# The sample rows' 256 keys chosen on 128 partitions instead of 32, with totals by TensorE and one bank for the attention's sums

## The reference, cut to what matters

```python
score = einsum('bth,bths->bts', wib * IDX_HEADS ** -0.5, relu(idx_s))
score = where(causal, score, NEG)
top_s, top_i = lax.top_k(score, n_sel)             # n_sel = 256
kvs = kv[b_ix, top_i]
s = einsum('btghd,btngd->btghn', qg, kvs[:, :, :, 0]) * scale
p = _masked_softmax(s, ok)
o = einsum('btghn,btngd->btghd', p, kvs[:, :, :, 1])
```

## Time and profile before

| | us |
|---|---|
| runs: median of 3 (lowest, highest) | 2315.91 (2314.22, 2325.44) |
| profiled execution: its own time | 2321.67 |
| profiled execution: its span | 2319.9 |
| PE busy in the span | 1865.5 (80%) |
| DVE busy in the span | 1210.8 (52%) |
| ACT busy in the span | 626.4 (27%) |

### The profile page before, as it was taken

How to read it: one execution, slowest core, us unless ns; L and a number is a source line. 1 busy time by engine, 2 the same in 40 slices (tenths; PEclk the granted TensorE clock), 3 DMA queues, 4 the chain that set the end, 5 groups by cost and what they waited for, 6 DMA issues and landing times. The chain is left out here.

```text
span 2319.9 us, 29122 instructions
## 1 busy us (share of the span) xinstructions
PE 1865.5 (80%) x11577; PEld 1283.2 (55%) x11577; DVE 1210.8 (52%) x2379; ACT 626.4 (27%) x1574; POOL 206.6 (9%) x190
## 2 busy tenths in 40 slices
PE   5589998969999667596899987978867667787595
PEld 2289998336666444384676644554542344444383
DVE  0231002757777652443223899946956998233443
ACT  0331121555666112002111000005633444222101
POOL 0033120000000531000011000000020000331000
PEclk9789999979999877598999999989987999898698
DMA  6321111400000554310111101100010000884301
GB/s 207 155 113 55 57 38 50 161 34 1 1 1 2 243 247 182 147 46 30 62 61 42 48 19 38 38 0 1 1 51 23 1 1 1 322 352 197 147 1 75
DMA packets 38450, 188.53 MB, mean 81 GB/s; under 512 B 8267, under 2 KB 8364, under 8 KB 21738
## 3 DMA queue, kind: packets, MB, share of 16 engines
q0 software_dynamic: 16912, 102.68, 11.3%
q1 hardware_dynamic: 21404, 83.98, 10.0%
HBM read 171.69 MB, written 19.12 MB: 82 GB/s over the span
## 5 line engine op out<-in xcount | busy, mean ns | idle before, releaser
L729 PE MATMUL banks<-hT,w_in 128*128 128x352 f32 x864 | 264.5, 465 | 39.9 <-DVE qdT L801 18.8
L729 PEld LDWEIGHTS banks<-hT,w_in 128*128 128x128 f32 x864 | 163.9, 192 | 138.5 <-DVE qdT L801 21.1
L2471 PE MATMUL banks<-w_out_parts,mix_parts 128*128 128x512 f32 (+1 forms) x864 | 204.8, 400 | 36.1 <-DVE w_out_parts L176 36.1
L2471 PEld LDWEIGHTS banks<-w_out_parts,mix_parts 128*128 128x128 f32 (+1 forms) x864 | 159.8, 186 | 83.5 <-DVE w_out_parts L176 40.4
L1304 ACT ACTIVATE nsa_p<-banks,nsa_negmax 128x512 f32<-128x512 f32 (+3 forms) x192 | 104.2, 557 | 94.0 <-DVE nsa_negmax L1223 94.0
L724 PE MATMUL banks<-hT_rest,w_in_high 128*128 128x352 f32 x384 | 124.0, 323 | 0.0
L724 PE MATMUL banks<-hT_high,w_in_high 128*128 128x352 f32 x384 | 124.0, 323 | 0.0
L724 PE MATMUL banks<-hT_high,w_in_rest 128*128 128x352 f32 x384 | 123.9, 323 | 0.0
L726 PE MATMUL banks<-w_in,hT 128*128 128x256 f32 (+3 forms) x576 | 118.9, 362 | 6.1 <-DMA w_in<-in_w_in 6.1
L1223 DVE TENSOR_REDUCE nsa_negmax<-banks 128x2 f32<-128x1024 f32 (+4 forms) x77 | 84.6, 1099 | 69.7 <-PE banks L1177 59.4
L853 ACT ACTIVATE mix<-banks 128x352 f32<-128x352 f32 x48 | 22.0, 465 | 348.4 <-PE banks L729 229.0
(11 more groups left out here) (525 smaller groups left out, 3566.4 us busy)
## 6 DMA issues: line engine op xcount, KB each, us to landing
w_in<-in_w_in SPq DMA_DIRECT2D x24, 1056.0 KB, 4.9
ada_w<-in_ada SPq DMA_DIRECT2D x24, 1024.0 KB, 4.9
w_out<-in_l_w_out SPq DMA_DIRECT2D x4, 2048.0 KB, 7.7
x_in<-in_x_prompt SPq DMA_DIRECT2D x1, 4096.0 KB, 15.0
nsa_ring<-in_state_l_win_kv POOLq DMA_DIRECT2D x8, 512.0 KB, 6.9
x_after<-in_x_prompt SPq DMA_DIRECT2D x1, 4096.0 KB, 17.8
x_mid<-x_after SPq DMA_DIRECT2D x8, 512.0 KB
x_after<-x_mid SPq DMA_DIRECT2D x1, 4096.0 KB, 17.9
```

The lines of the kernel that those rows point to most:

```text
L729: last = pe.matmul(bank[:, 0:cn], w[:, j % slots, a, m * P:(m + 1) * P], k.hT[:, a, c0:c0 + cn], start=(a == 0), stop=(a == KT - 1))
L2471: last = pe.matmul(k.bank[u % 4][0:n, :], lhs, rhs, start=a == 0 and x == 0, stop=a == KT - 1 and x == 2)
```

## The change

**Layout.** `sample_score` has 128 partitions and 544 columns: the quarter g of the 2048 past keys (512 keys) lies on partitions 32g to 32g+31, and the new keys on the last quarter's columns 512 to 543; the other quarters have -3e38 there. TensorE writes the sums of the heads to the partitions of their quarter (two products of 256 columns for one of 512), and VectorE's copies have 64 partitions and 256 columns.

**The choice** is the class `SampleChoice` in place of `top_mask`. A count runs over 544 columns on 128 partitions and gives a partial count of each quarter. A product with `mates` (1 where two partitions belong to one sample row) puts the sum of the four on every partition, in column 0 of `bank[7]`; VectorE reads it there in its next turn. The equal scores use `earlier` in the last product, so that quarters count the ones before them. `top_mask` stays for the prompt rows.

**The loop.** `attend_pairs` takes `beside` for `between`. With it, there is one bank of sums, `bank[6]`, and a tile's products wait for the close of the tile before. VectorE does the close and the step of the choice at the start of a turn, ahead of the maxima, and TensorE does the total behind the transposes.

```diff
-            k.sample_score = k.sb(ws, "idx_score_s", [NS, PAST + NS], side="right")
+            k.sample_score = k.sb(ws, "idx_score_s", [P, QUARTER + NS], side="right")
...
-            choice = top_mask(k, k.nc.vector, ws, "sample_top", [(k.sample_score[:, :], k.sample_sel[:, :])], TOPK, NS)
-            attend_pairs(k, "dsa", jobs, values, close, scale_heads, dve_copies=None, between=choice)
+            attend_pairs(k, "dsa", jobs, values, close, scale_heads, dve_copies=None, beside=SampleChoice(k, ws, k.bank[7]))
...
+    sums = 1 if beside is not None else 2
+    sum_bank = lambda i: k.bank[6 + i % sums]
...
-                    if i >= 2:
-                        pe.wait_ge(closed, i - 1)
+                    if i >= sums:
+                        pe.wait_ge(closed, i - sums + 1)
...
+                    if beside is not None and t < beside.rounds:
+                        beside.sum_quarters(pe, t)
                     if t - LAG - 1 >= 0:
                         add(t - LAG - 1)
...
+                    if sums == 1 and t - LAG - 2 in ends:
+                        end_tile(t - LAG - 2)
+                    next(steps, None)
                     if t < U:
                         maximum(t)
...
+    def sum_quarters(self, pe, n):
+        pe.wait_ge(self.counted, n + 1)
+        pe.matmul(self.total, (self.earlier if n == self.rounds - 1 else self.mates)[:, :, :].rearrange("p g n -> p (g n)"), self.seen[:, :],
+                  start=True, stop=True).then_inc(self.totalled, 1)
...
+        for bit in range(30, -1, -1):
+            link(dve.tensor_scalar(self.place[:, :], self.found[:, :], 1 << bit, None, ALU.bitwise_or))
+            link(dve.tensor_tensor(self.bits[:, :], self.place[:, :], self.flip[:, :], ALU.bitwise_xor))
+            count_of(ALU.is_ge, self.upper[:, :] if bit >= 16 else score, kth, self.mask[:, :])
+            yield
+            n += 1
+            dve.wait_ge(self.totalled, n)
+            link(dve.tensor_scalar(self.step[:, :], self.total, count, float(1 << bit), ALU.is_ge, ALU.mult))
+            link(dve.tensor_tensor(self.found[:, :], self.found[:, :], self.step[:, :], ALU.bitwise_or))
...
-                    pe.matmul(sum_bank(c)[0:NS, 0:width(c)], wsum[:, :], relu[:, c % 2, 0:width(c)], start=True, stop=True).then_inc(summed, 1)
+                    v = relu[:, c % 2, :].rearrange("k (j p) -> k j p", j=4)
+                    for side in range(2):
+                        quarter = 2 * (c // 2) + side
+                        last = pe.matmul(sum_bank(c)[quarter * NS:(quarter + 1) * NS, 0:256].rearrange("n (j p) -> n j p", j=4), wsum[:, :],
+                                         v[:, :, side * HD:(side + 1) * HD], start=True, stop=True, skip_group_check=True)
```

More of the change, by code:

```diff
@@ L65, in constants @@
     rows["cmp_seen"] = q >= CMP - 1
-    rows["idx_tail"] = NEG * ~((r32 // DS == q // DS) & (r32 % DS <= q % DS))
+    rows["idx_tail"] = NEG * ~((r32 // DS == q % NS // DS) & (r32 % DS <= q % DS))
     rows["causal"] = NEG * (c > q)
@@ L1062, in jobs_of, with attend_pairs @@
     return [range(4)] if n <= 512 + P else [range(0, 2), range(2, 4)]
-def attend_pairs(k, name, jobs, values, close, scale, maps=False, dve_copies=None, between=None):
+def attend_pairs(k, name, jobs, values, close, scale, maps=False, dve_copies=None, beside=None):
     nc = k.nc
     LAG, SLOTS, PIECES = 7, 9, 6
+    sums = 1 if beside is not None else 2
+    sum_bank = lambda i: k.bank[6 + i % sums]
     units, last_of = [], []
@@ L1199, in add @@
                     await_copies(pe, pieces_to[u])
-                    if i >= 2:
-                        pe.wait_ge(closed, i - 1)
+                    if i >= sums:
+                        pe.wait_ge(closed, i - sums + 1)
                     for c in range(pieces_from[u], pieces_to[u]):
                         for b, (g, x, y) in enumerate(pieces[c][1]):
-                            last = values(pe, jb, k.bank[6 + i % 2], g, jb["js"][un["xs"][x]], un["k0"] // P + y,
+                            last = values(pe, jb, sum_bank(i), g, jb["js"][un["xs"][x]], un["k0"] // P + y,
                                           pT[:, c % PIECES, b * P:(b + 1) * P], (i, g) not in begun)
@@ L1263, in factors, with end_tile @@
                         link(dve.tensor_tensor(s, e, total.unsqueeze(1).to_broadcast([P, 2, h]), ALU.mult))
+                def end_tile(u):
+                    dve.wait_ge(summed, u + 1)
+                    close(dve, ends[u], sum_bank(ends[u])).then_inc(closed, 1)
+                steps = beside.steps(dve) if beside is not None else iter(())
                 for t in range(U + LAG + 1):
+                    if sums == 1 and t - LAG - 2 in ends:
+                        end_tile(t - LAG - 2)
+                    next(steps, None)
                     if t < U:
@@ L1278, in _ @@
                                 copy_piece(dve, c)
[L1279 to L1289, removed]
+                    if sums == 2 and t - LAG - 2 in ends:
+                        end_tile(t - LAG - 2)
+                end_tile(U - 1)
+                for _ in steps:
+                    pass
             @block.scalar
@@ L1703 @@
 KEYS = 8
+QUARTER = PAST // 4
 HALVES = PAST // (P * KEYS)
@@ L2330, in add @@
                         pe.wait_ge(placed, c - 1)
-                    pe.matmul(sum_bank(c)[0:NS, 0:width(c)], wsum[:, :], relu[:, c % 2, 0:width(c)], start=True, stop=True).then_inc(summed, 1)
+                    if c == PIECES - 1:
+                        pe.matmul(sum_bank(c)[3 * NS:P, 0:NS], wsum[:, :], relu[:, c % 2, 0:NS], start=True, stop=True,
+                                  skip_group_check=True).then_inc(summed, 1)
+                        return
+                    v = relu[:, c % 2, :].rearrange("k (j p) -> k j p", j=4)
[3 more added lines that the diff above has]
+                                         v[:, :, side * HD:(side + 1) * HD], start=True, stop=True, skip_group_check=True)
+                    last.then_inc(summed, 1)
                 turn(0)
@@ L2374, in _ @@
                 last.then_inc(w_ready, 1)
+                dve.memset(k.sample_score[0:3 * NS, QUARTER:QUARTER + NS], TAKEN)
                 link(dve.memset(qz[:, :], 0.0))
```

66 lines of the change are left out of this document (61 added, 5 removed).

## The result

The changed kernel took 2249.55 us in the median of 4 runs (2248.01 to 2255.90), the kernel before 2315.30 beside it (2314.22 to 2325.44): 0.9712 of its time, 95% interval 0.9679 to 0.9745. The profiled execution took 2250.08 us, its span is 2248.2.

What follows compares the result with a forecast made beforehand. VectorE was taken to bound layer 1's attention while it chooses keys. Regular turns 31.7, filling 13 and last steps 7.7, less 0.5 and 1.5, gave 50.4, taken as 50 us: median 2315.91 to 2266 us, range 2252 to 2288.

Steps and rivals of the forecast that it cites:

- The count: VectorE's count per bit of the choice: 0.777 us at 544 elements instead of 2.37, 1.59 us less for each of 31 bits.
- Reading the bank: VectorE's read of the total from PSUM: costs nothing that counts, against the skill's estimate of 65 ns a read, 2.2 us.
- The regular turn: Turns 7 to 31 of layer 1's attention: 5.47 to 4.15 us each, 31.7 us gained over 24 turns (13.7 to 40).
- One bank: Waits at tile closes with a single bank of sums: 0.2 us in each of 7 closes, 1.5 us lost.
- The filling: First seven turns of the stage: seven narrower counts and passes moved ahead of the first maximum, 13 us gained (9 to 14).
- The last steps: The choice's last three turns: the scan and wide passes go, 4.15 us a turn instead of 20.2 in all, 7.7 gained.
- The next three turns: Turns behind the choice's last steps take over a scan, two passes and five copies: 0.5 us lost.
- The indexer: Sample rows' indexer ahead of the attention: smaller copies, three times late in its stage, gain 0.5 us, spent by the filling's setup.
- the rival in which TensorE hides everything: Totals slip into TensorE's gaps, a turn takes 3.8 us, the gain is 63 us, time 2253; chance 0.12.
- three signs of being wrong: Turn over 4.9 us; TensorE's count or VectorE's total waits over 0.5 us a turn; clock below 0.8 in turns 7 to 31.
- A chain through three engines: Total, count, maximum, exponential, copies and transposes follow each other every turn: 4.9 us a turn, 28 us gained, 2288; chance 0.14.
- The slow clock: TensorE at 1.2 GHz: a turn of some 7.25 us, 93 us lost against 50 gained if all 30 ran so, 2359; chance 0.04.

Runs made afterwards that it cites:

- the run with 544 keys: Kernel before, its choice made over only the first 544 of 2080 keys, on 32 partitions, with two banks and no totals: 2255.95 us, 0.9729 of before.
- the floor: Changed kernel without the whole choice of the sample rows' keys, two banks of sums, no totals: 2246.45 us, 0.9687 of before; turns 7 to 31 took 85.8 us.
- the run with two more operations: Changed kernel with the VectorE operation that sets the trial bit made three times instead of once: 2261.59 us, 0.9757 of before.
- the late close: Changed kernel, one bank of sums, with the close back at the end of VectorE's turn, behind the scaling: 2269.11 us, 0.9807 of before.
- the two bf16 runs: Changed kernel with partial counts, mates and earlier in bf16, so a total is one TensorE pass instead of two: 2255.57 us, and again 2255.71 us.

## Why the prediction was right or wrong

The sign and the cause (the width of the count) were right; the size was short by 12 us (62.3 against 50 in the profiles), and most of that lies in one step, the regular turn. The range's lower end was missed by 2.45 us in one series and not in the other, which is within the runs' scatter; the 2266 was missed in both.

**The count: right.** 0.777 us were forecast, 0.779 measured in all 31 bits; the stage's old 2.37 is gone, and the run with 544 keys shows that this alone brings nearly the whole gain. The four small operations, costed at nothing, grew by 0.01 to 0.02 each.

**Reading the bank: right.** The step from the bank took 0.151 us, `place` beside it from SBUF 0.154, and the step of the kernel before, from SBUF on 32 partitions, 0.142. The estimate of 65 ns more for each read by the Trainium skill (VectorE: DVE Perf Modes, section on the TRN2 errata) does not show here.

**The regular turn: this step failed.** It set the turn by TensorE, 3.69 + 0.25 for the total, and added 0.2 for what two level engines lose on each other: 4.15. Its three numbers were too large. The 3.69 was one full turn (with four score products of 256 columns in the earlier trace rows, not two); TensorE's mean over the stretch, with its shorter units, is 3.575, by the floor. The total costs 0.12, not 0.25, as long as its count is there. So TensorE needs some 3.70, an estimate from these two, and VectorE is the later: the run with two more operations, in whose list of waits VectorE has none, puts its own pace at 4.19 - 0.37 = 3.82, and the turn measured 3.87. The prediction's own figure for VectorE, 3.88, is within 0.01 of the measured turn. The loss of the two on each other is thus 0.05, not 0.2; layer 0's loop, where that came from, has TensorE as the busier engine and VectorE at 78%. 24 x 0.28 = 6.7 us of the shortfall.

**One bank: 1.5 us were charged, nothing was paid**, at the place that the close now has: 85.79 against 85.80 us without a choice, and with it no wait of TensorE for a close.

**The filling: right in its size**, 13.1 us for 13, and its new length 21.0 for 21. The granted clock rose there from 0.59 to 0.71, which the sum did not have; what that gave was not tested. **The last steps** gained 9.7 for 7.7, by the same wrong turn of 4.15: they take 3.48 us each, with TensorE busy 9.84 of 10.45. **The next three turns** gained 0.6 where 0.5 was to be lost. The scan, 1.29 us, already lies ahead of turn 34's maximum, and the passes and copies fill time in which VectorE had waited 3.5 us for scores and now waits for nothing. **The indexer** and its set-up were put at nothing together; they gained 0.45. **The drain and layer 0's attention** kept their lengths (19.4; 254.7 and 255.1 us from the first to the last maximum).

The sum with these numbers is 13.1 + 38.4 + 9.7 + 0.6 + 0.45 = 62.3 us. That is near the rival in which TensorE hides everything, which gave 3.8 us a turn, 63 us and 2253, at 12%. Its number came out partly by luck: its 3.8 was read from free turns that TensorE set, and VectorE's pace happens to be 3.82. The reason against it, that a share of the turns has a tile to close, doesn't hold: a close is 0.68 us of VectorE and no wait.

**What was to show it.** TensorE busy over 88% at a clock over 0.95: 92% at 1.00. ScalarE's waits for maxima halved: 72.2 to 34.6. No wait for totals or counts near 0.5 us a turn: none, and 0.07. Maxima 4.0 to 4.4 us apart: wrong, 3.87. The stage 168 us long: wrong, 154.7. None of the three signs of being wrong came, since all three stood on the slow side.

**The other rivals.** A chain through three engines was not there: VectorE never waited for a total. The slow clock did not come in the changed kernel's regular turns, in either profile (1.00 and 0.99 in turns 7 to 31). By the rule of the Trainium skill (TensorE: Matmul & The Clock Gate, section on a second HAM failure mode) it would have swung with these gaps. It fell to 0.50 once between turns 7 and 31 in three other profiles, those of the narrow count, of the late close and of one of the two bf16 runs, and in the last of these the slow turn took 1.6 us longer.

## What to carry to other kernels

When a change cut the engine that set this loop, the new turn came out near the larger of the two engines' own means over the stretch. Such a mean has the gaps between an engine's instructions in it (VectorE's 3.82 us, of which it is busy 3.65), and the next engine's has its short turns. Take a loss for two level engines only from a loop with the same bound; here the 0.2 us in place of 0.05 made 3.6 of the 12 us of error, and TensorE's 3.94 in place of VectorE's 3.82 another 2.9. To see which of two busy engines sets a turn, add a little work to one, take a little from the other, and compare turn by turn. A small product in the middle of TensorE's row of matmuls cost less than its own row shows (0.12 us for 0.28), with its operand there before its turn. The shared bank was free with the read that empties it first in VectorE's turn, and cost TensorE waits of up to 2.5 us with it last. Where whole runs of one kernel scatter by 13 us, compare the stage's lengths: in two kernels with a second profile they repeated within 0.1 us, in a third within 1.9, with the fall of the clock.

## What the runs showed of the hardware that had not been expected

A 128x1 product between transposes and value products put the latter off by 0.12 us in fp32 and by 0.01 in bf16, while its own rows last 0.28 and 0.17. The granted clock fell to 0.50 behind an idle time of 1.85 us in one profile and held 1.00 behind 1.86 in another of the same kernel. With the totals made twice, TensorE was busy 22.86 of 23.19 us of the filling and was granted 0.50 all through it, and 5.33 of 5.33 us of turn 7 behind it; why it was not granted more stays open.
